# Softmax rows divided by their sums on two engines: first head of a pair on VectorE, second on ScalarE

## What is computed

```python
admissible = (k_pos[None, :] // CHUNK) <= (q_pos[:, None] // CHUNK)
head_scores = relu(einsum('bthi,bsi->bths', q_idx, k_idx))
index_score = einsum('bth,bths->bts', w_idx, head_scores)
_, sel = lax.top_k(where(admissible, index_score, -inf), n_select)
logits = einsum('bthd,btkd->bhtk', q, k[sel]) * ATT_SCALE + rel_bias[t5_bucket(...)]
p = softmax(where(valid, logits, -inf), axis=-1)        # 8 heads
y_b = einsum('bhtk,btkd->bthd', p, v[sel])
```

## Time and profile before

| | us |
|---|---|
| median of 3 runs | 1057.68 |
| lowest and highest | 1056.74, 1057.71 |
| time of the profiled execution | 1056.88 |
| its span, from first to last instruction | 1055.1 |

### The profile page before, as it was taken

The page is one execution under the profiler, slowest core; times in us unless marked ns, Lnnn a source line. Parts: engine busy times, 40 slices in busy tenths (PEclk is TensorE's granted clock), DMA queues, the critical chain, the costliest instruction groups (busy, mean ns, idle before and its releaser), DMA issues.

```text
span 1055.1 us, 18633 instructions
## 1 busy us (share of the span) xinstructions
PE 1003.9 (95%) x7557; PEld 919.1 (87%) x7557; DVE 606.0 (57%) x1203; ACT 480.1 (46%) x824; POOL 498.6 (47%) x334
## 2 busy tenths in 40 slices
PE   1899999999999999999998999989999999999996
PEld 1789898878899999998777899977888999999975
DVE  6659997788983101101583899987898311100137
ACT  1355435667876322223124733466688542222210
POOL 2234455544564744445434174554455474445540
PEclk9999999999999999999999999999999999999999
DMA  6531453011112224323225223211111222352312
GB/s 198 192 102 46 146 165 126 2 41 41 41 41 81 80 81 161 100 81 120 91 68 195 76 91 113 82 58 42 41 41 42 72 65 80 100 184 81 106 55 90
DMA packets 70073, 95.44 MB, mean 90 GB/s; under 512 B 4458, under 2 KB 61252, under 8 KB 69348
## 3 DMA queue, kind: packets, MB, share of 16 engines
q1 hardware_dynamic: 66068, 82.68, 24.2%
q0 software_dynamic: 3488, 10.46, 2.9%
q10 hardware_dynamic: 432, 1.11, 0.3%
HBM read 79.46 MB, written 14.78 MB: 89 GB/s over the span
## 4 chain that ended last, share of the span: by engine, by line
PE 76%; DVE 15%; DMA 3%; issue 2%; ACT 2%; POOL 2%; SPq 0%; DVEq 0%; ACTq 0%; POOLq 0%
PE ps L514 35%; PE ps L861 10%; PE ps L812 10%; DVE attn L1346 3%; PE ps L727 3%; DVE top L1343 3%; PE ps L537 2%; PE ps L748 2%; PE ps L787 2%; PE ps L766 2%; PE ps L706 2%; DVE attn L1319 2%; DMA raw<-in_w_in 2%; DVE attn L1381 1%; DVE x_nat L1235 1%
## 5 line engine op out<-in xcount | busy, mean ns | idle before, releaser
L1566 POOL TENSOR_TENSOR w_lo<-raw,w_hi 128x1024 fp32r<-128x1024 f32 (+1 forms) x116 | 283.0, 2440 | 404.6 <-ACT w_hi L912 404.5
L514 PE MATMUL ps<-xT_hi,w_hi 128*128 128x288 f32 x864 | 256.1, 296 | 0.0
L514 PE MATMUL ps<-xT_hi,w_lo 128*128 128x288 f32 x864 | 254.5, 295 | 0.0
L514 PE MATMUL ps<-xT_lo,w_hi 128*128 128x288 f32 x864 | 254.5, 295 | 0.0
L912 ACT ACTIVATE w_hi<-raw 128x1024 fp32r<-128x1024 f32 (+1 forms) x116 | 121.2, 1046 | 107.2 <-PE ps L514 72.7
L1527 DVE TENSOR_TENSOR qy<-qy,ps 128x576 f32<-128x576 f32 x32 | 24.1, 754 | 253.8 <-PE ps L514 253.8
L514 PEld LDWEIGHTS ps<-xT_hi,w_hi 128*128 128x128 f32 x864 | 162.1, 188 | 1.3 <-issue 1.1
L514 PEld LDWEIGHTS ps<-xT_lo,w_hi 128*128 128x128 f32 x864 | 162.1, 188 | 0.0
L514 PEld LDWEIGHTS ps<-xT_hi,w_lo 128*128 128x128 f32 x864 | 162.0, 188 | 0.0
L961 ACT ACTIVATE qy<-ps,bias 128x576 f32<-128x576 f32 x34 | 25.2, 742 | 126.3 <-PE ps L514 126.2
L1657 POOL TENSOR_TENSOR attn<-attn 128x1024 f32<-128x1024 f32 (+1 forms) x24 | 54.2, 2259 | 59.2 <-DVE attn L1454 59.2
(11 more groups left out here) (202 smaller groups left out, 2300.3 us busy)
## 6 DMA issues: line engine op xcount, KB each, us to landing
raw<-in_w_in SPq DMA_DIRECT2D x44, 1024.0 KB, 5.2
raw<-in_w_out SPq DMA_DIRECT2D x8, 1024.0 KB, 5.0
x_kept<-x_nat SPq DMA_DIRECT2D x2, 2560.0 KB, 11.1
x_nat<-x_kept SPq DMA_DIRECT2D x2, 2560.0 KB, 11.2
raw<-in_w_proj_a SPq DMA_DIRECT2D x8, 512.0 KB, 3.5
raw<-in_w_proj_b SPq DMA_DIRECT2D x8, 512.0 KB, 4.7
x_nat<-in_x_prompt SPq DMA_DIRECT2D x4, 512.0 KB, 7.6
out<-stage POOLq DMA_DIRECT2D x8, 256.0 KB, 4.3
```

What stands on the lines that cost most here:

```text
L514: last = mm(out, a, b[:, HALF * half:HALF * (half + 1)], start=(k == 0 and i == 0), stop=(k == n - 1 and i == 2))
L1566: g.tensor_tensor(lo, src, hi.bitcast(f32), ALU.subtract).then_inc(s_lo, 1)
```

## The change

The division of a pair's two heads is split between two engines. VectorE still takes both reciprocals, and still multiplies the first head. The second head's multiplication becomes an ACTIVATE of the function Copy on ScalarE, with the reciprocal as a scale that is read from a [128, 1] column. It has its own semaphore, and the counts of `s_pn` go by pairs. On ScalarE `normalise_second(p-1)` stands after the exponential of the next pair's first head and ahead of the copy of transposed probabilities that followed it.

```diff
@@ transpose_probs (TensorE)
-                    pe.wait_ge(s_pn, L * N_B + s + 1)
+                    pe.wait_ge(s_pn2 if s % 2 else s_pn, L * NBP + s // 2 + 1)
@@ ScalarE, new
+                def normalise_second(p):
+
+                    ti, m = divmod(p, PAIRS)
+                    _, _, n, _, nk, _, _ = tile_of(*BT_ORDER[ti])
+                    c = 2 * p % P_SLOTS + 1
+                    act.wait_ge(s_ri, L * NBP + p + 1)
+                    act_f(prob[0:n, c, 0:nk], prob[0:n, c, 0:nk], ACT.Copy, scale=row_inv[0:n, c:c + 1]).then_inc(s_pn2, 1)
+
@@ ScalarE, the loop of rounds
                         for hh in range(2):
                             if p < NBP:
                                 exp_row(2 * p + hh)
+                            if hh == 0 and 1 <= p <= NBP:
+                                normalise_second(p - 1)
                             if r >= 1:
                                 move_probs(2 * p - 4 + hh)
@@ normalise (VectorE)
                     dve.wait_ge(s_ex, L * N_B + 2 * p + 2)
                     if 2 * p >= P_SLOTS:
-                        dve.wait_ge(s_pn, L * N_B + 2 * p - P_SLOTS + 2)
+                        dve.wait_ge(s_pn, L * NBP + p - P_SLOTS // 2 + 1)
+                        dve.wait_ge(s_pn2, L * NBP + p - P_SLOTS // 2 + 1)
                     v.reciprocal(row_inv[0:n, c:c + 2], row_sum[0:n, c:c + 2]).then_inc(s_ri, 1)
                     dve.wait_ge(s_ri, L * NBP + p + 1)
-                    for hh in range(2):
-                        x = prob[0:n, c + hh, 0:nk]
-                        v.tensor_scalar(x, x, row_inv[0:n, c + hh:c + hh + 1], None, ALU.mult).then_inc(s_pn, 1)
+                    x = prob[0:n, c, 0:nk]
+                    v.tensor_scalar(x, x, row_inv[0:n, c:c + 1], None, ALU.mult).then_inc(s_pn, 1)
```

More of the change, by code:

```diff
@@ L305, in build @@
         s_ri = sem("row_inv_ready")
-        s_pn = sem("prob_ready")
+        s_pn = sem("first_probs_of_pair_normalised")
+        s_pn2 = sem("second_probs_of_pair_normalised")
         s_pt = sem("prob_transposed")
```

## The result

The changed kernel takes 1060.18 us (median of 10 runs, 1057.68 to 1060.78), the kernel before 1056.76 beside it (median of 10; the three runs from which I forecast had 1057.68). The ratio is 1.0027 [1.0017, 1.0037]: slower by 0.3%. The forecast of 1057.0, its range up to 1059.2 and its sign are all wrong: I had 0.7 us less, and it is 3.4 more.

What follows compares the result with a forecast made beforehand. TensorE was taken to bound the kernel, with VectorE's relief counting only where it closes TensorE gaps. Gains of 0.2 and 0.4 less losses of 0.1 and 0.2 per layer made 0.7 us: 1057.7 - 0.7 = 1057.0 us, range 1054.6 to 1059.2.

Steps and rivals of the forecast that it cites:

- What bounds the kernel now: Prediction's opening: chain 76% on TensorE, 15% on VectorE; VectorE's relief counts only where it closes a TensorE gap.
- the clock is no term: Attention stage and stretch behind it: granted clock at full speed throughout the profile before, so no time assigned to it.
- Rounds 0 and 1: Gap at 182.08 shrinks by 0.8 us, the next transpose's gap gives back 0.6; gain 0.2 us per layer.
- Rounds 2 and 3: Second head's 2.60 us stall on VectorE goes, closing TensorE's 0.42 us gap at 200.41; gain 0.4 us per layer.
- The gap of 200.41: TensorE transpose waiting 0.42 us for ScalarE's copy of an earlier tile; forecast to close wholly.
- Rounds 5 to 7: Rounds 5 and 6 lose 0.1 us before the gap at 218.90; round 7's loop through ScalarE loses 0.2, per layer.
- The sum of a layer: All rounds of one layer's stage: 0.2 + 0.4 - 0.1 - 0.2, 0.3 to 0.4 us gained, both layers 0.7.
- The price of the copy: ScalarE's scaled copy, taken at the exponential's upper end: 0.61 us at 512 columns, 0.45 at 320.
- What would show it: Profile signs: 0.70 us copies, divisions about 12 us per layer's stage, ScalarE busy about 10 us more, TensorE idle nearly unchanged.
- A: Rival: copies hidden in ScalarE's pauses, VectorE's relief comes through, 1.7 us per layer, 1054.3 us; chance 0.22.
- B: Rival: loop over ScalarE becomes the bound in rounds of 512 and 320 columns, slower, 1060.1 us; chance 0.12.
- C: Rival: round 2's stall moves to the first head's division, losing round 3's 0.4 us; 1057.8 us; chance 0.06.

Runs made afterwards that it cites:

- experiment 9: Against the changed kernel, the scaled copy of every odd pair moved ahead of the next round's first exponential on ScalarE; 1053.98 us, 0.9979 of the kernel before.
- experiment 11: Against the changed kernel, odd pairs' copies ahead of the exponential plus a one-element VectorE memset behind each division; 1053.57 us, 0.9966 of the kernel before.
- experiment 3: Against the changed kernel, VectorE divides both heads as before and ScalarE makes its scaled copies on an unused tile; 1063.37 us, 1.0058 of the kernel before.
- experiment 8: Against the changed kernel, the scaled copy put one place later on ScalarE, behind the copy of transposed probabilities; 1061.41 us, 1.0043 of the kernel before.
- experiment 1: Against the changed kernel, eight useless matmuls of 288 columns per layer in TensorE's pause in round 1; 1057.17 us, 0.9996 of the kernel before.
- experiment 4: Against the changed kernel, pairs 0 to 2 of each layer divided on VectorE as before, split from pair 3; 1056.69 us, 1.0001 of the kernel before.
- experiment 10: Against the changed kernel, a one-element VectorE memset behind each of its 20 divisions per layer, restoring the instruction count; 1057.99 us, 1.0011 of the kernel before.

## Why the prediction was wrong

**The step that failed** is the sentence of "What bounds the kernel now" that says "the clock is no term". I had read it off a profile of the kernel before, where it was true, and carried it over to a kernel in which the sum itself made TensorE's pause in round 1 nearly twice as long. Two falls at 1.5 us are 3.0 of the 3.3 us between the profiles. That the filled pause brings the time back to 0.9996 with the transposes where they were, and that the changed kernel itself has a span of 1054.7 us in an execution without a fall, show this together; that the same fill one round later leaves three of five runs at a low clock speaks for it. The 1054.7 is close to my 1054.4 by luck: of the 0.4 us less than before, none comes from the two stages, which together are 0.17 longer. The Trainium skill (TensorE: Matmul & The Clock Gate, What's actually happening) says that what watches TensorE's activity runs free of the kernel's start, and that the point at which the clock changes varies for that reason. The 10 low and 7 higher runs of the changed kernel agree with that; no run here shows that it is the reason why a fall comes in one execution and not in another.

**Rounds 0 and 1: right.** Predicted gap 1.00 to 0.2, the one behind it 0.77 to 1.4, gain 0.2; measured 0.20, 1.37 and, at full clock, 0.33 less in the length of round 1 (8.57 to 8.24 us).

**Rounds 2 and 3: right.** The stall of 2.60 us on a second head is gone; the first head's division of that place takes its own time:

```profile
194.93 0.42 DVE L1392 TENSOR_SCALAR attn<-attn,row_inv 128x384 f32<-128x384 f32 x1
...
214.29 2.54 DVE L1392 TENSOR_SCALAR attn<-attn,row_inv 128x256 f32<-128x256 f32 x1
```

The gap of 200.41 has no row any more; round 3 is 0.30 us shorter (6.99 to 6.69) where 0.4 was predicted. The second line is the stall of a first head that I said would stay, and it stays.

**Rounds 5 to 7: right.** Predicted losses 0.1 and 0.2; round 6 is 0.15 longer and round 7 0.18. In round 7 the second transpose of a pair waits 0.16 us, as the prediction said. In round 6 the gap that it named, 0.61 us, stays as it was, and the loss stands one transpose ahead of it, a gap of 0.13 that becomes 0.28. Rounds 4, 8 and 9 move by 0.07 and less, round 5 by 0.02.

**The sum of a layer** was 0.35; layer 1 at full clock gives 0.26. It didn't hold for layer 2, which lost 0.43 instead, so that both layers made 0.2 us more where the sum had 0.7 less. This is a second step that failed, if a small one: I had counted the removed divisions only where they stood, but with 20 instructions fewer in layer 1 VectorE pauses in layer 2's index scores. With the count restored the stage of layer 2 gains 0.06.

**The price of the copy: right.** I took the exponential's length, near 0.70 us; it is 0.714 at 512 columns and 0.553 at 320 (exponential 0.718 and 0.560), and the next instruction starts 0.61 behind it. The Trainium skill (ScalarE: Activation LUTs, What ACT_TABLE_LOAD costs), with its charge for each pointer operand, had put it at the upper end as well, and the trace agrees.

**What would show it.** Divisions "about 12 us" was too low: 20 take 15.2, mean 759 ns against 644 before, because half of the count took away only one of the stalls. It cost nothing in time. ScalarE busy 10 us more: it is 8.5 in the window.

**The rivals.** A was wrong for this order of ScalarE, for the reason given against it, and right for another: experiment 9 has TensorE's gaps as with no copy at all, and with the count restored too (experiment 11) layer 2 gains 1.71 us, where A had 1.7. Of B the outward sign came true and the rest didn't: reciprocals wait 10.5 us for exponentials, against 2.4, and yet at full clock only rounds 6 and 7 are longer by more than 0.1 us, by the 0.15 and 0.18 named above. The time came out at B's 1060.1 by another mechanism, which is luck. Where the same copies stand without VectorE's relief (experiment 3) or one place later (experiment 8), ScalarE does hold up most rounds at full clock, so B was not far off. C didn't occur.

**What stays open.** What exactly makes the clock fall. The changed kernel fell behind 1.37 and 0.77 and in another execution did not; experiment 3 had 1.00, 1.38 and 0.77 in layer 1 without a fall and fell in layer 2 at the end of the 1.38; experiments 3 and 8, with gaps as long, have no run of 11 at 0.993 or less; experiment 11 fell behind a gap of 0.86 that every version has; and the fall at about 108 us, ahead of the change and behind a gap of 0.55 that all versions have, shows in the profiles of the changed kernel and of experiments 1, 3, 4, 8 and 10, not in the other six or in the kernel before. Which gaps count, over what stretch, and what differs between executions, no run here tells apart. Nor is it shown what VectorE's pause of 0.47 us is, or where it is when it isn't there: no like pause shows nearby in the profiles without it. Shown is only that it comes and goes with the number of instructions ahead.

## What to carry to other kernels

When the sum of an edit lengthens a pause of TensorE, even where it shortens another by more, weigh the clock as a rival of its own: here 0.6 us of longer pause cost 3 us in the profile and about as much in 10 of 17 runs, and the profile of before could not show it. Compare matmul counts at equal busy time, then look at the granted clock in windows of two microseconds, and test by filling the pause with useless matmuls, once in the pause and once behind it, and take their own time off the second. Look at whole stages in a profile without a fall as well: there the same copies cost anything from nothing to 5 us, by their place and by what VectorE had to do. An instruction moved to another engine belongs where that engine waits for something else: 0.7 us of copy in front of the instruction that TensorE waits for took back the whole gain, and the same copy one place earlier, for every other pair, was free.

## What the hardware showed that I had not expected

- Half a microsecond of idle time can decide how often the clock falls: with gaps of 0.84 and 0.77 us none of 11 runs is at 0.993 or less, with 1.37 and 0.77 it is 10 of 17. It isn't the length of a gap alone, as experiments 3 and 8 show. One fall lasts from 186.0 to 189.4 us and costs 1.5.
- Execution to execution the same program shows either; a single profile is no proof that a kernel's clock is full. One profiled execution of the changed kernel took 1060.2 us, another 1056.5.
- VectorE pauses 0.47 us between two like instructions when 20 instructions fewer stand ahead, and not when 17 fewer or as many as before do. Alone it is small, but it pushed one multiply-add from 0.20 us ahead of GpSimd's instruction to 0.16 behind its start. That one took 2.56 us in place of 0.54 and delayed top-k by 2.4.
